# A new prologue for a one-core hybrid decoder layer: parameter loads on another queue, paired column tiles, 32-bit gate rows

## The chip, the cores and the metric

The kernel runs on 1 core of one Trainium2 chip. The metric is the device time of one execution in microseconds; 3 runs of the kernel before gave a median of 978.57 (978.53 to 978.91). Below, TensorE is the matmul engine (PE, its weight loads PEld), VectorE is DVE, ScalarE is ACT, GpSimd is POOL and SyncE is SP; SPq and ACTq are the DMA issues of those engines. PSUM has 8 banks of 512 columns in float32.

## The reference

One layer, with x of 1024 rows by 1024 columns:

```python
mod = jax.nn.silu(c) @ w_ada + b_ada
shift, scale, gate = jnp.split(mod, 3, axis=-1)
h = x * (1.0 + scale[:, None, :]) + shift[:, None, :]
proj = h @ w_in + b_in           # q,k,v,z | q,k,v,o,z | i,f | merge gates
# branch A: causal stick-breaking attention, 8 heads x 64, SiLU gate, projection
# branch B: conv on q,k, chunkwise mLSTM, 4 heads x 128, with i and log f per row
log_f = jax.nn.log_sigmoid(ml_f.astype(jnp.float32)).transpose(0, 2, 1)
y = (jax.nn.sigmoid(g_sb) * y_sb + jax.nn.sigmoid(g_ml) * y_ml) @ w_out
return layer_norm(DEEPNORM_ALPHA * x + (1.0 + gate[:, None, :]) * y, ln_g, ln_b)
```

What matters here is the start: the columns of mod (a product of a 1024 vector with 2048 columns of w_ada), h transposed (features on partitions), and the first products of h with w_in, among them 8 rows for the gates i and f of the four mLSTM heads.

## The kernel before

All large products are split into three: a number is kept as a high part (fp32r, 32 bits rounded by the copy) and a low part (the rest), and hH x wH, hL x wH and hH x wL are summed in a bank. The feature axis is cut into 8 tiles of 128 (KT), named d or k; the rows into two halves of 512. Every engine has its own program, written by hand, with semaphores between them. An engine works strictly in the order of its program.

The prologue, to about 70 us, does the following for each tile d:

- SP (lines 423 to 463) issues the load of x's 128 columns (x_rows), two loads of 128 columns of w_ada (a_raw, shift and scale; three slots, A_BUFS), and pieces of the first weights: load g (pro_load) is 4 of the 8 feature tiles of group g % 3; group 0 is the 8 gate columns, 1 and 2 are sb_q and sb_k. Load 3 and later wait until VectorE has made the low part of load g - 3. Ahead of all this stand seven small parameter loads (prm).
- VectorE (ada_rows, L1333 to L1339) sums silu(c)[k] times a_raw's row k over k, in two accumulators of 256 columns, and adds them.
- TensorE (ada_columns, L653) turns the sum over partitions into a column by a product with ones; VectorE (mod_columns, L1368 and L1369) adds the bias.
- TensorE (turn_x, L665) transposes x, 8 blocks into two banks; ScalarE (shifted, L941 and L945) applies scale and shift into h_raw (two buffers) and makes hH; VectorE (low_h, L1362) makes hL.
- TensorE (tile_of, L615 to L617) adds tile k's products into six banks: three groups, two halves, three products each. Group 0 has only 8 output rows (w_proH, w_proL with 8 columns).
- ScalarE and VectorE split each weight load into high part (L925) and low part (L1354), in pro_split(g).

TensorE's order is turn_x(d), tile_of(d - 1) of groups 0 and 1, ada_columns(d + 1), tile_of(d - 1) of group 2. After the last tile ScalarE moves the gate rows (r_if, L958), SP copies them to 4 partition groups with four loads of r_f and four of r_i (L467 and L469), and a chain of ScalarE and VectorE work on the rows begins. ScalarE then moves next_q and next_k out of the banks. The following products (project, L637) are jobs 3 and 4, then the loop over the four heads; job 3 writes the bank that next_q is read from.

## Time and profile before

| | |
|---|---|
| median of 3 runs | 978.57 us (978.53 to 978.91) |
| profiled execution | 978.23 us, of it the span 976.4 us |
| TensorE busy | 941.4 us (96%) |
| VectorE, ScalarE, GpSimd busy | 599.7 (61%), 454.3 (47%), 166.9 us (17%) |
| moved | 73.96 MB, mean 76 GB/s |
| chain that ended last | PE 83%, DVE 9%, the rest 2% or less each |

The page divides the span into 40 slices: TensorE is at 9 tenths in all but the first and the last, the DMA engines are at 9 in the first two only. In a timeline a row merges instructions of one kind that follow each other (x says how many): its two numbers are the start and the time from the first one's start to the last one's end. Matmuls are pipelined: one lasts some 0.4 us, but the next starts 0.23 us later, so starts are compared, not durations.

### The profile page before, as it was taken

The numbers are of one execution on the slowest core, as the hardware profiler recorded it, in microseconds if no ns is written. First come the engines' busy times: TensorE is split into PE (matmuls) and PEld (weight loads), VectorE is DVE, ScalarE is ACT, GpSimd is POOL, SyncE is SP. The second block draws the span as 40 slices with busy tenths as digits, with TensorE's granted clock in tenths as the row PEclk, the third lists the DMA queues.
The fourth block names the chain that finished last, engine by engine and source line by source line (L and its number), as shares of the span: only waits on it lengthen the run. The fifth ranks groups of instructions, "written<-read, shape, count | busy, mean of one in ns | idle before, by whom it ended". The sixth has DMA issues, their size and how long they took to land.

```text
span 976.4 us, 13097 instructions
## 1 busy us (share of the span) xinstructions
PE 941.4 (96%) x4965; PEld 757.3 (78%) x4965; DVE 599.7 (61%) x1144; ACT 454.3 (47%) x813; POOL 166.9 (17%) x138
## 2 busy tenths in 40 slices
PE   1999999999999999999999999999999999999996
PEld 1677878888778888778888778788888888878885
DVE  4857785666775757866657857543653333345996
ACT  2454575553665544665644756433843232242100
POOL 1010122240132430123220133311100000001200
PEclk9999999999999999999999999999999999999999
DMA  9932211102202012111113101115721221315232
GB/s 230 291 92 56 68 30 44 33 23 67 74 23 55 22 44 79 42 44 34 35 31 98 44 22 45 33 44 188 243 65 43 57 63 45 96 44 183 87 130 86
DMA packets 99561, 73.96 MB, mean 76 GB/s; under 512 B 4616, under 2 KB 90760, under 8 KB 99500
## 3 DMA queue, kind: packets, MB, share of 16 engines
q1 hardware_dynamic: 94828, 58.44, 22.2%
q0 software_dynamic: 2368, 8.41, 2.6%
q10 hardware_dynamic: 2304, 6.29, 1.7%
q8 instruction: 39, 0.64, 0.3%
q14 instruction: 22, 0.18, 0.1%
HBM read 64.59 MB, written 8.40 MB: 75 GB/s over the span
## 4 chain that ended last, share of the span: by engine, by line
PE 83%; DVE 9%; SPq 2%; ACT 2%; DMA 2%; issue 1%; DVEq 0%; ACTq 0%
PE bank L637 41%; PE bank L617 9%; PE bank L615 9%; PE bank L616 9%; PE bank L758 4%; PE bank L742 3%; DMA a_raw<-in_w_ada 2%; PE bank L731 2%; DVE m_q L1548 2%; DVE wL L1345 1%; PE bank L771 1%; SPq L454 1%; DVE m_q L1560 1%; PE bank L714 1%; PE bank L732 1%
## 5 line engine op out<-in xcount | busy, mean ns | idle before, releaser
L637 PE MATMUL bank<-hH,wH 128*128 128x512 f32 x688 | 274.8, 399 | 0.6 <-DVE wL L1345 0.6
L637 PE MATMUL bank<-hL,wH 128*128 128x512 f32 x688 | 272.9, 397 | 0.0
L637 PE MATMUL bank<-hH,wL 128*128 128x512 f32 x688 | 269.2, 391 | 0.0
L575 POOL TENSOR_TENSOR ez<-ez,rem 128x512 f32<-128x512 f32 (+3 forms) x96 | 136.0, 1436 | 411.2 <-DVE rem L1497 411.2
L637 PEld LDWEIGHTS bank<-hH,wH 128*128 128x128 f32 x688 | 129.1, 188 | 38.4 <-issue 10.7
L1345 DVE SCALAR_TENSOR_TENSOR wL<-w_raw,wH 128x512 fp32r<-128x512 f32 x116 | 87.6, 760 | 114.1 <-ACT wH L917 113.6
L637 PEld LDWEIGHTS bank<-hH,wL 128*128 128x128 f32 x688 | 129.4, 188 | 26.6
L637 PEld LDWEIGHTS bank<-hL,wH 128*128 128x128 f32 x688 | 129.4, 188 | 24.6 <-issue 1.0
L917 ACT ACTIVATE wH<-w_raw 128x512 fp32r<-128x512 f32 x116 | 72.5, 627 | 98.0 <-PE bank L617 71.1
L1497 DVE TENSOR_TENSOR_SCAN rem<-rem,ones 128x512 f32<-128x512 f32 (+3 forms) x96 | 88.6, 964 | 38.7 <-ACT rem L1019 38.7
L1006 ACT ACTIVATE ez<-bank 128x512 f32<-128x512 f32 (+3 forms) x96 | 41.8, 488 | 95.2 <-PE bank L733 95.2
L1481 DVE TENSOR_SCALAR ez<-ez 128x512 f32<-128x512 f32 (+3 forms) x80 | 27.5, 344 | 53.7 <-ACT ez L1006 52.7
L616 PE MATMUL bank<-hL,wH 128*128 128x512 f32 x144 | 56.2, 390 | 0.0
L615 PE MATMUL bank<-hH,wH 128*128 128x512 f32 x144 | 56.2, 390 | 0.0
L617 PE MATMUL bank<-hH,wL 128*128 128x512 f32 x144 | 56.0, 389 | 0.0
L1015 ACT ACTIVATE rem<-ez 128x512 f32<-128x512 f32 (+3 forms) x96 | 45.0, 517 | 7.2 <-DVE ez L1484 7.1
L604 POOL TENSOR_TENSOR yL<-yT,yH 128x1024 fp32r<-128x1024 f32 x4 | 9.6, 2396 | 207.5 <-ACT yH L1274 207.5
L1019 ACT ACTIVATE rem<-rem 128x512 f32<-128x512 f32 (+3 forms) x96 | 44.4, 510 | 0.0
L1027 ACT ACTIVATE at<-bank 128x512 f32<-128x512 f32 (+3 forms) x96 | 41.2, 482 | 5.6 <-PE bank L742 5.6
L758 PE MATMUL bank<-at,v_tok 128*64 128x128 f32 x576 | 42.0, 281 | 0.0
L742 PE MATMUL bank<-ident,ez 128*128 128x128 f32 x288 | 39.2, 272 | 0.0
L742 PEld LDWEIGHTS bank<-ident,ez 128*128 128x128 f32 x288 | 34.3, 140 | 6.1
(240 smaller groups left out, 1517.6 us busy)
## 6 DMA issues: line engine op xcount, KB each, us to landing
w_raw<-in_w_in SPq DMA_DIRECT2D x104, 256.0 KB, 2.9
a_raw<-in_w_ada SPq DMA_DIRECT2D x16, 512.0 KB, 7.3
x_rows<-in_x SPq DMA_DIRECT2D x8, 512.0 KB, 6.4
raw<-in_w_ada POOLq DMA_DIRECT2D x8, 512.0 KB, 4.7
x_in<-in_x SPq DMA_DIRECT2D x8, 512.0 KB, 4.2
out_y<-res SPq DMA_DIRECT2D x7, 512.0 KB, 2.9
raw<-in_w_out SPq DMA_DIRECT2D x10, 256.0 KB, 3.9
m_w<-bm_scratch ACTq DMA_DIRECT2D x4, 512.0 KB, 4.0
```

What stands on the lines that cost most here:

```text
L575: g.tensor_tensor(e, e, r, ALU.mult).then_inc(a_done[h], 1)
L615: t.matmul(ps, aH, bH, start=k == 0, stop=False)
L616: t.matmul(ps, aH, bL, start=False, stop=False)
L617: return t.matmul(ps, aL, bH, start=False, stop=k == kt - 1)
L637: ins = t.matmul(banks(number)[half][:], w, a, start=(r == 0), stop=(r == JOB_MM // 2 - 1))
L742: ins = t.transpose(z_ps[h][:, b * P:(b + 1) * P], ez[s % 2][h][:, b * P:(b + 1) * P], ident[:])
L758: ins = t.matmul(y_ps[64 * h:64 * h + 64, tt], v_tok[:, j, 64 * h:64 * h + 64], at_sb[h][:, b * P:(b + 1) * P], start=b == 0 and not conti ...
L917: a.activation(wH[:, slot, :, 0:width], w_raw[:, slot, :, 0:width], ACT.Copy, scale=scale)\
L1015: a.activation(rem[s % 2][h][:, 0:w], ez[s % 2][h][:, 0:w], ACT.Ln, bias=1.0).then_inc(ln_done[h], 1)
L1019: a.activation(r, r, ACT.Exp, scale=-1.0).then_inc(rem_done[h], 1)
L1345: v.scalar_tensor_tensor(out=wL[:, slot, :, 0:width], in0=w_raw[:, slot, :, 0:width], scalar=scale, in1=wH[:, slot, :, 0:width], op0=ALU.m ...
L1497: v.tensor_tensor_scan(back, back, ones[:, 0:1].to_broadcast((P, w)), first, ALU.mult, ALU.min)\
```

## The change

- The seven parameter loads are issued by ScalarE ahead of its table load, no longer by SP.
- The tiles form five blocks, [0], [1], [2, 3], [4, 5], [6, 7]. x and w_ada are loaded by block: 256 columns at a time for the pairs, w_ada in two pieces of four k each. ada_rows, ada_columns and mod_columns work by block, 512 wide for a pair.
- The gate rows (group 0) are no longer split products: w_if holds the 8 columns for all k, and gate_rows(d) multiplies them with h_raw in 32 bits, one product for each half; the halves' results stand in one bank, at partitions 0 to 7 and 32 to 39 (two column groups).
- low_h moves between the halves of a block's sums; the low parts of weight loads 3 to 5 are made behind mod_columns of block 2. TensorE's order is new.
- VectorE copies half 1 of the gate rows to partitions 0 to 7 before ScalarE adds the bias. The four r_i loads are issued by ScalarE, right behind r_if and ahead of next_q; the four r_f loads stay on SP.

The new `gate_rows`, the block loops and the orders, from the diff (`ada_pieces(b)` gives number, slot and k range of a block's pieces; `ada_freed(n)` is the count of sums that frees piece n's slot; `pro_slot(g)` only renumbers buffers):

```diff
 PRO_CHUNKS = 2 * PRO_K
+BLOCKS = [[0], [1], [2, 3], [4, 5], [6, 7]]
+BLOCK_OF = [b for b, tiles in enumerate(BLOCKS) for _ in tiles]
 A_BUFS = 3
...
-        pro_ps = [[y_ps[0:2 * NH, :], misc_ps[2][0:2 * NH, :]],
+        pro_ps = [[y_ps[32 * half:32 * half + 2 * NH, :] for half in range(2)],
                   [proj_ps[half][:] for half in range(2)], [z_ps[half][:] for half in range(2)]]
...
+            for b, tiles in enumerate(BLOCKS):
+                cols_b = slice(tiles[0] * P, (tiles[-1] + 1) * P)
+                sp.dma_start(x_rows[:, :, cols_b], x_v[:, :, cols_b]).then_inc(x_cols_in[b], 16)
+                for number, slot, lo, hi in ada_pieces(b):
+                    if number >= A_BUFS:
+                        sp.wait_ge(ada_used, ada_freed(number))
+                    piece = a_raw[:, slot].rearrange("p (k w c) -> p k w c", k=hi - lo, w=2)
+                    for what in range(2):
+                        sp.dma_start(piece[:, :, what], w_ada_w[:, lo:hi, what, cols_b]).then_inc(a_in[slot], 16)
+                for g in {0: range(3), 2: range(3, PRO_CHUNKS)}.get(b, ()):
+                    pro_load(g)
...
-                pe.wait_ge(x_cols_in[d], 16)
+                b = BLOCK_OF[d]
+                pe.wait_ge(x_cols_in[b], 16)
+                pe.wait_ge(mod_done, 2 * BLOCKS[b][-1] + 2)
...
+            def gate_rows(d):
+                for n in range(2):
+                    pe.wait_ge(m_drained[n], d + 2 - n)
+                if d % 4 == 0:
+                    pe.wait_ge(wL_done, PRO_K * (d // 4) + 1)
+                for half in range(2):
+                    ins = t.matmul(pro_ps[0][half], w_if[:, d], h_raw[:, d % 2, halves(half)], start=d == 0,
+                                   stop=d == KT - 1, skip_group_check=True)
+                    if d == KT - 1:
+                        ins.then_inc(filled[half], 1)
+                    elif half:
+                        ins.then_inc(if_used, 1)
...
             ada_columns(0)
-            for d in range(KT):
-                turn_x(d)
-                if d:
-                    tile_of(d - 1, 0, PRO_K - 1)
+            turn_x(0)
+            gate_rows(0)
+            for d in range(2):
+                tile_of(d, 1)
+                ada_columns(d + 1)
+                tile_of(d, 2)
+                turn_x(d + 1)
+                gate_rows(d + 1)
+            for d in range(2, KT):
                 if d + 1 < KT:
-                    ada_columns(d + 1)
-                if d:
-                    tile_of(d - 1, PRO_K - 1, PRO_K)
-            tile_of(KT - 1, 0, PRO_K)
+                    turn_x(d + 1)
+                tile_of(d, 1)
+                tile_of(d, 2)
+                if d % 2 == 0 and d + 2 < KT:
+                    ada_columns(d // 2 + 2)
+                if d + 1 < KT:
+                    gate_rows(d + 1)
...
                 if d > 1:
                     act.wait_ge(hL_done, d - 1)
+                    act.wait_ge(if_used, d - 1)
...
-                        bias_copy(r_if[0:2 * NH, halves(half)], half, n,
-                                  r_bias[0:2 * NH, :], pro_ps[0][half])
+                        else:
+                            act.wait_ge(if_moved, 1)
+                        rows = r_if[0:2 * NH, halves(half)]
+                        bias_copy(rows, half, n, r_bias[0:2 * NH, :], rows if half else pro_ps[0][half])
...
                         pro_split(g)
+                if n == 0:
+                    for half in range(2):
+                        act.wait_ge(drained[half], 1)
+                    for q in range(4):
+                        act.dma_start(r_i[32 * q:32 * q + NH, :], r_if[0:NH, :]).then_inc(rows_in, 16)
...
+            ada_rows(0, 0, KT)
+            mod_columns(0)
+            for g in range(3):
+                pro_split(g)
+            for b in range(1, len(BLOCKS)):
+                ada_rows(b, 0, KT // 2)
+                low_h(b - 1 if b < 3 else 2 * b - 4)
+                ada_rows(b, KT // 2, KT)
+                if b > 2:
+                    low_h(2 * b - 3)
+                mod_columns(b)
+                if b == 2:
+                    for g in range(3, PRO_CHUNKS):
                         pro_split(g)
-                elif d < 4:
-                    pro_split(d + 2)
-            low_h(KT - 1)
+            for d in range(KT - 2, KT):
+                low_h(d)
+            dve.wait_ge(filled[1], 1)
+            dve.wait_ge(rows_zero, 5)
+            v.tensor_copy(r_if[0:2 * NH, halves(1)], pro_ps[0][1]).then_inc(if_moved, 1)
```

How the instructions stand, at three places. First VectorE, from the low part of tile 1 to that of tile 2. The kernel before (a_raw the columns of w_ada, a_acc their sums, ada_in the slots' loads):

```order
L1362 TENSOR_TENSOR hL<-h_raw,hH 128x1024 [waits hH_done]
L1368 TENSOR_TENSOR mod<-bank,cols 128x1 [waits ada_done]
L1369 SCALAR_TENSOR_TENSOR mod<-bank,cols 128x1
L1354 SCALAR_TENSOR_TENSOR w_proL<-w_raw,w_proH 128x512 [waits wH_done]
L1333 TENSOR_SCALAR a_acc<-a_raw,silu_c 128x256 [waits ada_done,ada_in0]
L1333 TENSOR_SCALAR a_acc<-a_raw,silu_c 128x256
L1336 SCALAR_TENSOR_TENSOR a_acc<-a_raw,silu_c,a_acc 128x256 [waits ada_used] x6
L1339 TENSOR_TENSOR a_acc<-a_acc 128x256 [waits ada_used]
L1362 TENSOR_TENSOR hL<-h_raw,hH 128x1024 [waits hH_done]
```

The change, from the fifth of the eight wide sums (tiles 2 and 3):

```order
L1395 SCALAR_TENSOR_TENSOR a_acc<-a_raw,silu_c,a_acc 128x512 [waits ada_used,ada_in0]
L1395 SCALAR_TENSOR_TENSOR a_acc<-a_raw,silu_c,a_acc 128x512 [waits ada_used] x3
L1400 TENSOR_TENSOR a_acc<-a_acc 128x512 [waits ada_used]
L1430 TENSOR_TENSOR mod<-bank,cols 128x1 [waits ada_done]
L1432 SCALAR_TENSOR_TENSOR mod<-bank,cols 128x1
L1430 TENSOR_TENSOR mod<-bank,cols 128x1
L1432 SCALAR_TENSOR_TENSOR mod<-bank,cols 128x1
L1414 SCALAR_TENSOR_TENSOR w_proL<-w_raw,w_proH 128x512 [waits wH_done] x2
L1392 TENSOR_SCALAR a_acc<-a_raw,silu_c 128x512 [waits ada_in1,ada_done]
L1392 TENSOR_SCALAR a_acc<-a_raw,silu_c 128x512
L1395 SCALAR_TENSOR_TENSOR a_acc<-a_raw,silu_c,a_acc 128x512 [waits ada_used] x2
L1424 TENSOR_TENSOR hL<-h_raw,hH 128x1024 [waits hH_done]
```

hL of tile 2 (the last row of both) stood behind the sums of tile 3 alone; it now stands behind the low parts of loads 4 and 5 (the row x2) and half of the sums of tiles 4 and 5. The low part of load 5 waits for wH_done, which ScalarE gives. hL of tile 1 now stands ahead of these rows, behind the fourth wide sum.

Second ScalarE, in the change alone, from tile 0's hH to tile 3's h_raw:

```order
L994 ACTIVATE hH<-h_raw 128x1024 [waits misc_drained1,misc_drained0]
L974 ACTIVATE w_if<-w_raw 128x32 [waits weights_in0]
L990 ACTIVATE h_raw<-bank,mod 128x512 [waits misc_filled0,mod_done]
L990 ACTIVATE h_raw<-bank,mod 128x512 [waits misc_filled1]
L994 ACTIVATE hH<-h_raw 128x1024 [waits misc_drained1,misc_drained0]
L974 ACTIVATE w_proH<-w_raw 128x512 [waits weights_in1]
L990 ACTIVATE h_raw<-bank,mod 128x512 [waits if_used,misc_filled0,hL_done,mod_done]
L990 ACTIVATE h_raw<-bank,mod 128x512 [waits misc_filled1]
L994 ACTIVATE hH<-h_raw 128x1024 [waits misc_drained1,misc_drained0]
L974 ACTIVATE w_proH<-w_raw 128x512 [waits weights_in2]
L990 ACTIVATE h_raw<-bank,mod 128x512 [waits if_used,misc_filled0,hL_done,mod_done]
```

At the end of the prologue, in the change:

```order
L1007 ACTIVATE r_if<-bank,r_bias 8x512 [waits proj_filled0,rows_zero,bias_in]
L1007 ACTIVATE r_if<-r_if,r_bias 8x512 [waits proj_filled1,if_moved]
L1043 DMA r_i<-r_if 4x1024 [waits proj_drained1,proj_drained0]
L1043 DMA r_i<-r_if 4x1024 x3
L1007 ACTIVATE next_q<-bank,cols 128x512 [waits proj_filled0]
L1007 ACTIVATE next_q<-bank,cols 128x512 [waits proj_filled1]
L1007 ACTIVATE next_k<-bank,cols 128x512 [waits proj_filled0]
```

The kernel before has the same rows up to h_raw of tile 3. There load 3 (w_if here, w_proH there) was issued right behind the columns of tile 1; it now stands behind the loads of the whole pair. At the end, these stood behind each other before:

```order
L958 ACTIVATE r_if<-bank,r_bias 8x512 [waits proj_filled0,rows_zero,bias_in]
L958 ACTIVATE r_if<-bank,r_bias 8x512 [waits proj_filled1]
L958 ACTIVATE next_q<-bank,cols 128x512 [waits proj_filled0]
L958 ACTIVATE next_q<-bank,cols 128x512 [waits proj_filled1]
L958 ACTIVATE next_k<-bank,cols 128x512 [waits proj_filled0]
L958 ACTIVATE next_k<-bank,cols 128x512 [waits proj_filled1]
```

Four DMA issues came in between r_if and next_q.

Third TensorE. The kernel before, the end of tile 1 to the start of tile 2:

```order
L616 MATMUL bank<-hL,w_proH 128x512
L617 MATMUL bank<-hH,w_proL 128x512
L665 MATMUL bank<-ident,x_rows 128x128 [waits mod_done,x_cols_in2]
L665 MATMUL bank<-ident,x_rows 128x128 x3
L665 MATMUL bank<-ident,x_rows 128x128 [waits misc_drained1]
L665 MATMUL bank<-ident,x_rows 128x128 x3
L615 MATMUL bank<-hH,w_proH 8x512 [waits hL_done]
L616 MATMUL bank<-hL,w_proH 8x512
L617 MATMUL bank<-hH,w_proL 8x512
```

The change, the same stretch (L678 transposes, L689 gate rows, L627 to L629 split products, L666 column sums):

```order
L629 MATMUL bank<-hH,w_proL 128x512
L678 MATMUL bank<-ident,x_rows 128x128 [waits misc_drained0,mod_done,x_cols_in2]
L678 MATMUL bank<-ident,x_rows 128x128 x3
L678 MATMUL bank<-ident,x_rows 128x128 [waits misc_drained1]
L678 MATMUL bank<-ident,x_rows 128x128 x3
L689 MATMUL bank<-h_raw,w_if 8x512 [waits misc_drained1,misc_drained0]
L689 MATMUL bank<-h_raw,w_if 8x512
L678 MATMUL bank<-ident,x_rows 128x128 [waits misc_drained0,mod_done,x_cols_in2]
L678 MATMUL bank<-ident,x_rows 128x128 x3
L678 MATMUL bank<-ident,x_rows 128x128 [waits misc_drained1]
L678 MATMUL bank<-ident,x_rows 128x128 x3
L627 MATMUL bank<-hH,w_proH 128x512 [waits hL_done]
L628 MATMUL bank<-hL,w_proH 128x512
```

Transposes and gate rows of tile 2 and transposes of tile 3 now come before the first split product of tile 2.

## Rows read from the trace of the kernel before

**Rows 1.** The page, busy us, share of the span, instructions.
```profile
PE 941.4 (96%) x4965; PEld 757.3 (78%) x4965; DVE 599.7 (61%) x1144; ACT 454.3 (47%) x813; POOL 166.9 (17%) x138
```

**Rows 2.** Waits, TensorE, 66 to 240 us: total us, times, longest.
```profile
PE bank L637 <- DVE wL L1345: 0.6, 1, 0.6
```

**Rows 3.** DMA view, 0 to 100 us: busy tenths in 40 slices of 2.5.
```profile
DMA  0199999999999999999999100041153000302240
```

**Rows 4.** Windows: length, busy us of each engine, clock, DMA share, GB/s.
```profile
45.00:50.00 5.00, 5.00 (x30) 3.86 (x28) 4.26 (x13) 1.99 (x4) 0.00 (x0) 1.00 1.17 291
...
944.00:948.00 4.00, 4.00 (x19) 3.21 (x18) 2.59 (x4) 0.00 (x0) 0.00 (x0) 1.00 0.77 260
```

**Rows 5.** Timeline, SP's DMA issues: start us, us, what.
```profile
0.81 0.41 SPq L431 DMA_DIRECT2D prm<-in_c  x1
...
3.48 0.43 SPq L450 DMA_DIRECT2D x_rows<-in_x  x1
```

**Rows 6.** Timeline, VectorE at the start; in brackets idle time and what ended it.
```profile
7.00 0.17 DVE L1321 TENSOR_TENSOR silu_c<-cols,small 128x8 f32<-128x8 f32 x1
...
11.39 0.61 DVE L1333 TENSOR_SCALAR a_acc<-a_raw,silu_c 128x256 f32<-128x256 f32 x2 [4.22 <-DMA a_raw<-in_w_ada]
...
19.02 0.62 DVE L1333 TENSOR_SCALAR a_acc<-a_raw,silu_c 128x256 f32<-128x256 f32 x2 [1.55 <-DMA a_raw<-in_w_ada]
```

**Rows 7.** Timeline, TensorE: tile 0, tile 2, the one wait, job 3.
```profile
26.11 0.63 PE L616 MATMUL bank<-hL,w_proH 128*8 128x512 f32 x1
...
26.54 0.63 PE L617 MATMUL bank<-hH,w_proL 128*8 128x512 f32 x1
...
37.48 0.48 PE L615 MATMUL bank<-hH,w_proH 128*8 128x512 f32 x1
...
41.60 0.61 PE L653 MATMUL bank<-ones,a_acc 128*128 128x1 f32 x4 [1.08 <-DVE a_acc L1339]
...
69.30 0.39 PE L637 MATMUL bank<-hH,wH 128*128 128x512 f32 x1
```

**Rows 8.** Timeline, TensorE, tile 4: transposes, gate products, first 128-wide.
```profile
49.06 1.04 PE L665 MATMUL bank<-ident,x_rows 128*128 128x128 f32 x8
49.85 0.48 PE L615 MATMUL bank<-hH,w_proH 128*8 128x512 f32 x1
...
51.31 0.40 PE L615 MATMUL bank<-hH,w_proH 128*128 128x512 f32 x1
```

**Rows 9.** DMA issues, 0 to 100 us: count, KB each, median us to landing.
```profile
r_bias<-in_b_in POOLq DMA_DIRECT2D x1, 0.0 KB, 4.6
```

**Rows 10.** Timeline, VectorE's and ScalarE's steps for a tile and a load.
```profile
27.76 0.62 ACT L925 ACTIVATE w_proH<-w_raw 128x512 fp32r<-128x512 f32 x1
...
49.56 2.46 DVE L1336 SCALAR_TENSOR_TENSOR a_acc<-a_raw,silu_c,a_acc 128x256 f32<-128x256 f32 x6
...
49.78 1.45 ACT L941 ACTIVATE h_raw<-bank,mod 128x512 f32<-128x512 f32 x2 [2.92 <-PE bank L665]
51.32 1.06 ACT L945 ACTIVATE hH<-h_raw 128x1024 fp32r<-128x1024 f32 x1
...
52.41 1.23 DVE L1362 TENSOR_TENSOR hL<-h_raw,hH 128x1024 fp32r<-128x1024 f32 x1
...
64.55 1.89 DVE L1345 SCALAR_TENSOR_TENSOR wL<-w_raw,wH 128x512 fp32r<-128x512 f32 x3
```

**Rows 11.** Timeline, TensorE: 32-bit products in two column groups, and the next.
```profile
403.28 0.44 PE L758 MATMUL bank<-at,v_tok 128*64 128x128 f32 x4
403.65 0.45 PE L731 MATMUL bank<-kH,qH 64*128 64x384 f32 x2
```

**Rows 12.** Timeline, the gate rows' copies and issues; ScalarE's own DMA issue.
```profile
66.09 1.29 ACT L958 ACTIVATE r_if<-bank,r_bias 8x512 f32<-8x512 f32 x2 [1.15 <-PE bank L617]
...
70.08 2.44 SPq L469 DMA_DIRECT2D r_i<-r_if  x4
...
107.93 0.34 ACTq L1139 DMA_DIRECT2D m_w<-bm_scratch  x1
```

More of the change, by code:

```diff
@@ L127, with pro_slot, ada_pieces, ada_freed @@
 PRO_CHUNKS = 2 * PRO_K
+BLOCKS = [[0], [1], [2, 3], [4, 5], [6, 7]]
+BLOCK_OF = [b for b, tiles in enumerate(BLOCKS) for _ in tiles]
 A_BUFS = 3
 Y_BUFS = 4
+def pro_slot(g):
+    return (g // PRO_K) * (PRO_K - 1) + g % PRO_K - 1
+def ada_pieces(b):
+    if b < 2:
+        return [(b, b, 0, KT)]
+    return [(2 * b - 2 + part, (2 * b - 2 + part) % A_BUFS, part * KT // 2, (part + 1) * KT // 2) for part in range(2)]
+def ada_freed(number):
+    before = number - A_BUFS
+    return 8 * (before + 1) if before < 2 else 16 + 4 * (before - 1)
 def segments():
@@ L467, in _ @@
                 sp.dma_start(r_f[32 * q:32 * q + NH, :], r_if[NH:2 * NH, :]).then_inc(rows_in, 16)
-            for q in range(4):
-                sp.dma_start(r_i[32 * q:32 * q + NH, :], r_if[0:NH, :]).then_inc(rows_in, 16)
             off = dict(zip(("mlq", "mlk", "mlv", "mlo", "mlz"), OFF_ML)) |\
@@ L905, in _ @@
             a = nc.scalar
+            bi = b_in[0]
+            rows = [
+                (ROW_C, c[0]), (ROW_ADA, b_ada[0]), (ROW_B, bi[0:OFF_IF]),
+                (ROW_GSB, bi[OFF_GSB:OFF_GSB + 2 * D]), (ROW_CB, conv_b[0]), (ROW_NG, ml_norm_g[0]),
+            ]
+            for row, src in rows:
+                src = src.rearrange("(t p) -> t p", p=P)
+                act.dma_start(prm[row:row + src.shape[0], :], src).then_inc(params_in, 16)
+            act.dma_start(prm[ROW_CW:ROW_CW + 4 * KT, :], conv_w[0].rearrange("j (t p) -> (j t) p", p=P))\
+                .then_inc(params_in, 16)
             a.preload_act_table_set("natural_log_exp_and_others")
@@ L987, in _ @@
                         pro_split(g)
+                if n == 0:
+                    for half in range(2):
+                        act.wait_ge(drained[half], 1)
+                    for q in range(4):
+                        act.dma_start(r_i[32 * q:32 * q + NH, :], r_if[0:NH, :]).then_inc(rows_in, 16)
                 if n == 2:
@@ L1323, in _, with ada_rows @@
             dve.wait_ge(silu_done, 1)
-            def ada_rows(d):
-                dve.wait_ge(a_in[d % A_BUFS], 32 * (d // A_BUFS + 1))
-                if d > 1:
-                    dve.wait_ge(ada_done, d - 1)
-                for k in range(KT):
-                    acc, row = a_acc[:, d % 2, k % 2], a_raw[:, d % A_BUFS, k]
+            def ada_rows(b, lo, hi):
+                if lo == 0 and b > 1:
+                    dve.wait_ge(ada_done, b - 1)
+                width = len(BLOCKS[b]) * P
+                for k in range(lo, hi):
+                    for number, slot, first, _ in ada_pieces(b):
+                        if k == first:
+                            dve.wait_ge(a_in[slot], 32 * (number // A_BUFS + 1))
+                    acc, row = a_acc[:, b % 2, k % 2, :, 0:width], ada_rows_of(b, k)
                     if k < 2:
```

125 lines of the change are left out of this document (52 added, 73 removed).

## Prediction

> **What bounds the kernel now.** I read the page first: TensorE is busy nearly all of the span of 976.4 us, so a change of its prologue counts by how much later or earlier TensorE starts its steady work [rows 1]. I take "job 3" (the first product of L637, at 69.30) as the end of the prologue and ask when it starts in the changed kernel. From the waits of TensorE behind it comes one more term, 0.6 us for VectorE's wL (L1345) [rows 2].
>
> Next the DMA digits and the windows: from 5 to about 54 us the DMA engines are saturated [rows 3], at 290 GB/s with rows of 512 bytes [rows 4]. SP issues the seven parameter loads first; x starts at 3.48 instead of 0.81 [rows 5]. The first two column tiles of w_ada are in at 11.39 and 19.02; silu(c) had been ready since 7.2 [rows 6]. Then TensorE: its products begin at 25.5, at first 0.43 us apart where later ones are 0.233 apart, as the lower of its two clock levels, 1.2 GHz, would give; tile 2 begins at 37.48, and between there and 69.30 it waits only once, for 1.1 us at 41.6 (the load of tile 4) [rows 7]. So from tile 2 on the prologue is 31.8 us of almost solid TensorE work. One tile of it: transposes 0.79, six 8-wide gate products 1.46 (0.233 each, and 0.06 that the first waits behind the transposes), twelve 128-wide ones 2.8, column sums about 0.5 [rows 7, 8].
>
> **The change, part by part.**
>
> *Parameters on ScalarE.* The big loads start 2.67 us earlier (0.81 for 3.48) [rows 5]. The parameters now travel beside them. Lower end: they are in as before. Upper end: r_bias, which did travel beside them, took 4.6 us to land [rows 9]; issued until 3.4, they are in at 8.0, silu(c) at 10.2, 1.5 us after tile 0's columns (11.39 - 2.67 = 8.7). The chain below has 1 to 2 us of slack there (ScalarE waits for a load until 26.2), so I price it at 0, at most 1.
>
> *Pairs.* Tiles 2 and 3 become one block. Tile 1's columns are in at 19.02 - 2.67 = 16.3. Behind them come x of two tiles and two pieces of w_ada, 3 x 1.05 MB. At 290 GB/s this takes 10.9 us. Rows of 1024 bytes may go faster: at 4 KB rows the engines moved 260 GB/s at a share of 0.77, 338 per unit of share, against 290/1.17 = 248 [rows 4]. I take 340 GB/s, between 290 and 395 (338 x 1.17), nearer to 512 bytes: 9.3 us, second piece in at 25.6; ends 24.3 and 27.2. The row shows that longer rows are cheaper. The Trainium skill ("DMA: Bandwidth & Descriptors", Specifications) asks for 512 B or more for line rate; by that rule the pairs would gain nothing and my sum would be 1.6 us higher. The trace disagrees in part: 512-byte rows stay at 290.
>
> *The chain to tile 2's products.* The third gate load (16 KB) is queued behind both pieces, and ScalarE's w_if copy of it stands in front of tile 1's h_raw: about 26.2. Then ScalarE: copy 0.3, h_raw 1.55, hH 1.15 (with gaps) -> 29.2 [rows 10]. VectorE has low_h(1) ahead of the second half of the block's sums: 1.14; four wide steps. A 256-wide step is 0.41, a 512-wide operation of the same kind 0.63 [rows 10]; at 0.66 four are 2.6; the wide final sum 0.7 (low_h, 1024 wide, takes 1.22) -> 33.6. TensorE's columns and the four mod operations 1.2 -> 34.9, while TensorE does tile 1's second product (1.4) -> transposes of tile 2 at 35.9. Then 0.7, h_raw 1.55, hH 1.15 -> 39.3, and now the order of the change matters: VectorE has mod, then the low part of weight load 5, then the first half of the next block, and only then low_h(2). Load 5's high part stands on ScalarE behind hH(2): 0.62 -> 39.95; VectorE 0.7, two wide TENSOR_SCALARs 0.42 and two steps 0.66 (2.2), low_h(2) 1.3 -> **44.1**. Before, tile 2 began at 37.5: 6.6 us later. Both waits can be read in the order of the instructions, they are no estimate; TensorE idles some 3.5 us here.
>
> *TensorE from tile 2 to job 3.* Six tiles x 12 x 0.233 = 16.8; four sets of transposes 3.5; two sets of eight column sums 1.2; one wait for VectorE's sums 0.6; five gate rows. A gate row is two 32-bit products, 512 wide, in two column groups. The nearest row is L758: two such products, 128 wide, are followed by the next work after 0.37 us [rows 11]; a 128-wide 32-bit transpose takes 0.79/8 = 0.10 [rows 8], and each of the two rounds is 384 columns longer (0.32): 1.0, with the change of mode 1.1. Lower end 0.95 (no such loss), upper end no overlap at all, 1.95. The row shows two groups starting together. The Trainium skill ("TensorEngine Tiling (Array Packing)", Key Properties) says that a change of tiling mode drains the engine; without any drain the sum would be 0.1 us less a row. Five rows: 5.5. Together 27.6 against 31.8: **-4.2**.
>
> *Copy of the rows, r_i on ScalarE's queue.* Gate row 7 now ends 2.8 us before job 3 could start (call that J), the rows' chain moves up. But ScalarE has, in this order: three weight copies until J - 2.35, r_if half 0 and half 1 (0.65 each) until J - 1.0, four r_i issues, and only then next_q, whose bank job 3 writes. An issue of r_i takes 0.58 + 0.04 on SP, 2.44 for four; ScalarE's own issue of m_w took 0.34 [rows 12]. With 0.61: J + 1.5, next_q's first half 0.7 (and 0.1) -> J + 2.3. TensorE waits **+2.3**; with 0.34 each, +1.2.
>
> *Behind it.* The rows' chain reaches VectorE relatively 3 us earlier, so the wait of 0.6 for wL goes [rows 2]: **-0.6**. The two others of 0.6 and 0.7 in the first iteration are VectorE's conv work, which follows TensorE: 0.
>
> **Sum:** 6.6 - 4.2 + 2.3 - 0.6 = +4.1 us. Against the profiled execution's 978.23 it is 982.3; the median of the runs is 0.34 above that, so 982.7.
>
> **Rivals.**
> 1. *The pairs cost by number, not by size* (the other side). Where a wide VectorE operation costs what a narrow one does, the four steps, the sum and the next block's half take 1.75 us less, and with loads at 395 GB/s another 1.3: tile 2 at 41.0, sum +1.0, 979.6. This mechanism makes the kernel faster where tile 2 starts before 40.0 (37.5 + 4.2 - 2.3 + 0.6); with tile 2 at 38.0, hardly later than before, the sum is 0.5 - 4.2 + 2.3 - 0.6 = -2.0, 976.6. For it: a narrow operation has a fixed share in its 0.41. Against it: the 1024-wide one takes 1.22, and the two waits that the order fixes are left. 8 in 100 for all of it.
> 2. *No wait at job 3*: ScalarE's issues are cheap or next_q is early: 1.2 to 2.3 less, 980.4 to 981.6. For it the row of 0.34, against it that r_i's shape cost 0.58. 15 in 100.
> 3. *The column groups do not overlap*, 1.95 instead of 1.1 a gate row, five times: +4.2, 986.9. Against it: L758's pairs. 8 in 100.
> 4. *Loads gain nothing from longer rows* (the rule above, here as a mechanism): second piece and third gate load 1.6 us later, 984.3. 15 in 100.
> 5. *TensorE falls to the slower clock* in its idle stretches before 44: each product then costs 0.2 more for a few us: +1 to +2, 984.2. For it: tile 0's products 0.43 apart after an idle stretch. 10 in 100.
> The forecast itself: 44 in 100.
>
> **How the numbers follow.** The likeliest time is 982.7. A measurement of this kernel tells about 0.2% from no change, 976.6 to 980.5. Faster: the far end of rival 1, 0.06. Within: the rest of 1, the low part of 2, and errors of the chain of over 2 us, 0.15. Slower 0.79. The range of 979.0 to 987.0 takes in rivals 2 to 5 and leaves out most of rival 1 and combinations of 3 with 4 or 5.
>
> **What would show it.** The third gate load's copy on ScalarE near 26; VectorE waiting some 4 us for wH of load 5, until about 40; tile 2's first product (L627) near 44; gate rows of 1.1 us (start to next start); four r_i issues on ScalarE ahead of next_q, and L649's first product 2 us after L629's last; behind it no wait for wL. The forecast is wrong if tile 2 starts before 41, or if the gate rows cost below 0.8 us.

## The result, and the profile after

| | before | changed |
|---|---|---|
| median of the runs | 978.55 us (978.26 to 978.91) | 986.31 us (984.98 to 987.99) |
| single runs, granted clock | all within 0.7 us | 985.02 (0.993), 984.98 (0.993), 987.60 (0.990), 987.99 (0.986) |
| profiled execution, its span | 978.23, 976.4 us | 985.02, 983.3 us |
| job 3 starts | 69.30 | 77.02 |

The change makes the kernel slower: the ratio of the times is 1.0082, 95% interval 1.0069 to 1.0094. The runs of the kernel before agree to 0.07%; those of the changed kernel are 3 us apart, the slower ones with the lower mean clock of TensorE. The profiled execution, on which the readings below rest, is one of the two faster runs.

The page of the changed kernel, busy us, share of the span, instructions; this answers to [rows 1]:

```profile
PE 942.7 (96%) x4949; PEld 755.7 (77%) x4949; DVE 596.4 (61%) x1116; ACT 454.1 (46%) x813; POOL 167.0 (17%) x138
```

TensorE is busy 1.3 us longer, though it has fewer instructions; the rest of the 6.9 us by which the span grew is idle time. Job 3 comes 7.7 us later, so all of the loss lies in the prologue, and 0.8 us came back behind it. The windows of the prologue (us, busy us of PE, PEld, DVE, ACT, POOL, granted clock, DMA share, GB/s), against 290 GB/s in [rows 4]:

```profile
20.00:30.00 10.00, 7.45 (x30) 5.16 (x28) 5.82 (x13) 3.25 (x5) 0.00 (x0) 1.00 1.13 329
30.00:40.00 10.00, 6.68 (x28) 5.14 (x28) 4.71 (x11) 1.45 (x2) 0.00 (x0) 0.83 1.10 348
40.00:50.00 10.00, 6.40 (x27) 4.49 (x27) 8.30 (x12) 4.08 (x5) 0.00 (x0) 0.83 0.61 190
50.00:60.00 10.00, 10.00 (x57) 6.96 (x56) 7.27 (x16) 5.02 (x6) 0.00 (x0) 1.00 0.17 51
```

While they run the loads are faster. They stand still from 42 to 45 us (0 GB/s in windows of 1 us), where SP waits for a slot of a_raw, and end near 52, where those of [rows 3] went on to 55. TensorE is idle for a third of the time from 30 to 50, and its clock is 0.83 there. One caution on the clock column: up to about 24 us it reads 1.00 although tile 0's products are 0.43 us apart (20.71 to 23.44), and it does so in the kernel before too; in that stretch the spacing tells the level and the column does not. TensorE's rows of that stretch (start, us, what, in brackets the idle time before it and what ended it), for [rows 7]:

```profile
33.84 1.05 PE L666 MATMUL bank<-ones,a_acc 128*128 128x1 f32 x8 [1.71 <-DVE a_acc L1400]
34.76 0.65 PE L627 MATMUL bank<-hH,w_proH 128*128 128x512 f32 x1
...
37.34 1.51 PE L678 MATMUL bank<-ident,x_rows 128*128 128x128 f32 x8
40.11 1.03 PE L689 MATMUL bank<-h_raw,w_if 128*8 128x512 f32 x4 [1.25 <-ACT h_raw L990]
...
45.66 0.79 PE L627 MATMUL bank<-hH,w_proH 128*128 128x512 f32 x1 [3.50 <-DVE hL L1424]
...
48.39 0.47 PE L627 MATMUL bank<-hH,w_proH 128*128 128x512 f32 x1
...
50.73 1.03 PE L689 MATMUL bank<-h_raw,w_if 128*8 128x512 f32 x4
51.70 1.09 PE L678 MATMUL bank<-ident,x_rows 128*128 128x128 f32 x8
...
77.02 0.47 PE L649 MATMUL bank<-hH,wH 128*128 128x512 f32 x1 [2.36 <-ACT next_q L1007]
```

Tile 2 starts at 45.66 (37.48 before), behind 3.50 us of waiting for hL; the six products from 34.76 (to 37.34) and the first six of tile 2 (to 48.39) are 0.43 us apart, the spacing of the lower clock; a gate row takes 0.97 us (50.73 to 51.70); job 3 waits 2.36 us for next_q. VectorE and ScalarE say why hL of tile 2 is late:

```profile
35.20 0.68 DVE L1414 SCALAR_TENSOR_TENSOR w_proL<-w_raw,w_proH 128x512 fp32r<-128x512 f32 x1
41.66 0.69 DVE L1414 SCALAR_TENSOR_TENSOR w_proL<-w_raw,w_proH 128x512 fp32r<-128x512 f32 x1 [5.78 <-ACT w_proH L974]
42.27 0.87 DVE L1392 TENSOR_SCALAR a_acc<-a_raw,silu_c 128x512 f32<-128x512 f32 x2
43.07 1.40 DVE L1395 SCALAR_TENSOR_TENSOR a_acc<-a_raw,silu_c,a_acc 128x512 f32<-128x512 f32 x2
44.39 1.22 DVE L1424 TENSOR_TENSOR hL<-h_raw,hH 128x1024 fp32r<-128x1024 f32 x1
...
40.05 1.06 ACT L994 ACTIVATE hH<-h_raw 128x1024 fp32r<-128x1024 f32 x1
41.02 0.61 ACT L974 ACTIVATE w_proH<-w_raw 128x512 fp32r<-128x512 f32 x1
```

VectorE stands 5.78 us at the low part of load 5, whose high part ScalarE makes only behind hH of tile 2, then works on the next block, and only then makes the hL that TensorE waits for. At the other end of the prologue:

```profile
72.66 0.73 ACT L1007 ACTIVATE r_if<-r_if,r_bias 8x512 f32<-8x512 f32 x1
73.47 2.68 ACTq L1043 DMA_DIRECT2D r_i<-r_if  x4
73.74 2.76 SPq L481 DMA_DIRECT2D r_f<-r_if  x4
76.19 1.27 ACT L1007 ACTIVATE next_q<-bank,cols 128x512 f32<-128x512 f32 x2 [2.81 <-issue]
80.68 1.06 ACT L1046 ACTIVATE r_e<-r_f 128x1024 f32<-128x1024 f32 x1 [2.06 <-DMA r_f<-r_if]
```

The four r_i issues keep ScalarE for 2.7 us, 0.67 each (0.61 on SP in [rows 12]). The rows are in 7.3 us after r_if ends at 73.39; before it was 6.9 us (67.38 to 74.25). Two queues brought nothing here; why the second queue did not help is not shown.

### The profile page after: what moved, and what is told of

It reads as the page before. It is cut to its first block, busy times and chain, and to the rows that moved or that the text cites. A ratio compares the mean times of both kernels' runs of the same rounds, so it can differ in the third digit from the quotient of the medians.

```text
span 983.3 us, 13050 instructions
## 1 busy us (share of the span) xinstructions
PE 942.7 (96%) x4949; PEld 755.7 (77%) x4949; DVE 596.4 (61%) x1116; ACT 454.1 (46%) x813; POOL 167.0 (17%) x138
## 4 chain that ended last, share of the span: by engine, by line
PE 85%; DVE 10%; ACT 3%; issue 1%; ACTq 1%; DMA 1%; POOL 0%; DVEq 0%; POOLq 0%
PE bank L649 42%; PE bank L627 9%; PE bank L629 9%; PE bank L628 9%; PE bank L792 4%; PE bank L776 3%; PE bank L765 2%; DVE m_q L1619 1%; PE bank L805 1%; DVE m_q L1631 1%; DVE wL L1405 1%; PE bank L748 1%; PE bank L766 1%; PE bank L767 1%; PE bank L810 1%
## 5 line engine op out<-in xcount | busy, mean ns | idle before, releaser
L649 PEld LDWEIGHTS bank<-hH,wH 128*128 128x128 f32 x688 | 129.1, 188 | 40.2 <-issue 13.5
L627 PE MATMUL bank<-hH,wH 128*128 128x512 f32 x144 | 56.2, 390 | 0.0
L629 PE MATMUL bank<-hH,wL 128*128 128x512 f32 x144 | 56.0, 389 | 0.0
```

What stands on the lines that cost most here:

```text
L627: t.matmul(ps, aH, bH, start=k == 0, stop=False)
L629: return t.matmul(ps, aL, bH, start=False, stop=k == kt - 1)
L649: ins = t.matmul(banks(number)[half][:], w, a, start=(r == 0), stop=(r == JOB_MM // 2 - 1))
```

## The experiments

All times are medians. The experiments ran on four chips; the kernel before, run beside each of them, had 978.15 to 978.40 us, so medians from different chips can be compared to some 0.4 us. An interval is given where the comparison is with the kernel before.

### The changed kernel, one cause at a time

**r_i back on SP.**

```diff
+            for q in range(4):
+                sp.dma_start(r_i[32 * q:32 * q + NH, :], r_if[0:NH, :]).then_inc(rows_in, 16)
...
-                    for q in range(4):
-                        act.dma_start(r_i[32 * q:32 * q + NH, :], r_if[0:NH, :]).then_inc(rows_in, 16)
```

> The changed kernel, with the four r_i issues back on SP behind the four of r_f. Theory (the issues stand ahead of next_q and cost TensorE its 2.36 us wait at job 3; the rows arrive no later, since 6.9 us passed between r_if and the rows before and 7.3 us now): the wait for next_q at L649 falls below 0.3 us, the rows are in at most 0.5 us later, a wait for wL of up to 0.7 us may come back; 1.5 to 2.4 us faster than the changed kernel, some 984.2 us. Rival (TensorE has a second reason to wait there, or the rows' chain becomes late): the wait moves to another line and less than 1 us is gained.

Measured: 982.87 us (982.43 to 988.47), ratio to before 1.0059 [1.0038, 1.0081]; the median is 3.4 us below the changed kernel's, more than expected. Four runs have a clock of 0.994 (982.4 to 985.0); the profiled one, 988.47, has 0.990. The wait for next_q is gone. In its place, the timeline of ScalarE and TensorE some 15 us later, and the window behind it:

```profile
82.91 1.06 ACT L1043 ACTIVATE r_e<-r_f 128x1024 f32<-128x1024 f32 x1 [5.07 <-DMA r_i<-r_if]
...
92.34 0.50 PE L651 MATMUL bank<-hH,wH 128*128 128x512 f32 x1 [1.86 <-DVE wL L1402]
```

```profile
92.00:96.00 4.00, 3.66 (x11) 2.93 (x12) 3.93 (x6) 0.00 (x0) 0.00 (x0) 0.67 0.25 66
```

The rows arrive as late as with two queues, 7.3 us after r_if (75.57 to 82.91). But the wait for wL is 1.86 us, where at most 0.7 was expected, and the clock behind it is 0.67. So by the waits of this one profile the issues cost TensorE 2.36 us and hid 1.86, and undoing them alone is worth 0.5 us. The runs show more: three of them lie at 982.4 to 982.9 where the changed kernel's two best have 985.0, at nearly the same mean clock. This isn't settled, since mean clocks do not say where the slow stretches lay.

**Low parts of loads 3 to 5 behind block 3.**

```diff
-                if b == 2:
+                if b == 3:
                     for g in range(3, PRO_CHUNKS):
                         pro_split(g)
```

> The changed kernel, with the low parts of weight loads 3 to 5 made behind mod_columns of block 3 instead of block 2, so that hL of tile 2 no longer stands behind the wait for load 5's high part. Theory (this order fixes tile 2's start at 45.66): tile 2 starts at 42 to 42.8, some 3 us earlier, and the kernel gains 2.7 to 3.4 us, up to 4.5 if TensorE then stays at the higher clock; about 983 us. Rival (tile 2 waits for the loads, the sums or h in any case): tile 2 starts later than 44.5 and less than 1.2 us is gained. Second rival (the low parts of loads 3 to 5 then come too late for tile 4's products): a wait at tile 4's first product takes back over 1 us.

Measured: 984.07 us (980.47 to 984.38), 2.2 us faster than the changed kernel where 2.7 to 3.4 were expected. The profiled run, 980.47 at a clock of 0.995, is 4.5 us faster than the changed kernel's profiled one; the other three have 0.988 and 984.0 to 984.4. TensorE's timeline:

```profile
29.77 0.72 PE L627 MATMUL bank<-hH,w_proH 128*128 128x512 f32 x1 [1.28 <-DVE hL L1424]
30.30 0.63 PE L628 MATMUL bank<-hL,w_proH 128*128 128x512 f32 x1
30.72 0.63 PE L629 MATMUL bank<-hH,w_proL 128*128 128x512 f32 x1
...
40.23 0.50 PE L627 MATMUL bank<-hH,w_proH 128*128 128x512 f32 x1 [0.26 <-DVE hL L1424]
```

Tile 2 starts at 40.23, 5.4 us earlier, with 0.26 us of waiting for 3.50; the rival (it waits in any case) falls, and no wait at tile 4 takes its place. The shorter wait alone makes 3.2 us. The rest is the clock: tile 1's second products and the transposes behind them were at the higher level here (1.6 us), and the clock had risen earlier in tile 0, so that tile 1's h_raw starts 0.7 us earlier. Tile 1's first products, on the other hand, were at the lower level (30.30 to 30.72), behind the same 1.28 us wait behind which the changed kernel kept the higher one (at 30.46).

**Fillers against the clock.**

```diff
+            def fill(n):
+                for _ in range(n):
+                    t.matmul(misc_ps[2][:], w_proH[:, 0, 0], hH[:, 0, halves(0)], start=True, stop=True,
+                             skip_group_check=True)
```

> The changed kernel, with 31 more 512-wide products (8 rows of nothing that is read: they go into a bank that no one reads then) in TensorE's idle stretches of the prologue: 6 before the column sums of tiles 2 and 3, 4 before each of two pairs of gate rows and 4 behind one, 13 before the first product of tile 2. Nothing else moves. Theory (part of the prologue's time is the lower clock that TensorE is granted behind its idle stretches, 0.43 us a product instead of 0.233): the products of tile 1 and of tile 2 run 0.23 apart, the kernel gains 1.5 to 2.9 us although it does more, and its runs lie closer together than the 3 us of the changed kernel's; about 984 us. Rival (the lower clock only fills time in which TensorE would wait for VectorE anyway, and the fillers stand in the way): no change or up to 2 us slower.

The fillers are full 128-row products. Measured: 984.05 us, four runs from 983.79 to 984.28, clock 0.995 in each. It does 31 products more and is 2.3 us faster at the median; the spread of 3 us is gone. Profile against profile it is only 0.7 us faster (984.28 against 985.02). Windows, and then TensorE's timeline at the two starts:

```profile
30.00:40.00 10.00, 9.20 (x50) 6.56 (x50) 4.61 (x12) 3.02 (x4) 0.00 (x0) 1.00 1.10 349
40.00:50.00 10.00, 9.22 (x48) 6.52 (x47) 9.96 (x19) 2.54 (x4) 0.00 (x0) 1.00 0.79 242
...
70.00:80.00 10.00, 7.64 (x27) 5.80 (x26) 1.92 (x4) 5.24 (x8) 0.00 (x0) 0.83 0.41 92
```

```profile
43.87 0.50 PE L627 MATMUL bank<-hH,w_proH 128*128 128x512 f32 x1 [0.48 <-DVE hL L1433]
...
74.52 0.47 PE L649 MATMUL bank<-hH,wH 128*128 128x512 f32 x1 [2.36 <-ACT next_q L1016]
```

At the higher clock tile 2 starts at 43.87 and job 3 at 74.52, within 0.5 us of what the prediction's chain gives (44.1 and 74.0). Behind the 2.36 us wait at job 3, which had no filler, the clock now fell (0.83), which it did not in the changed kernel's profile. From job 3 to the end of the span it is 907.9 us here and 906.3 there: 1.6 of the 2.5 us that job 3 gained are lost again. The changed kernel's profile is the exception: in all four other profiles with that wait (low parts behind block 3, fillers, one column group, parameters on SP) job 3's first products are 0.43 us apart, and it is 907.8 to 907.9 us from there to the end.

**Both halves of a gate row in one column group.**

```diff
-        pro_ps = [[y_ps[32 * half:32 * half + 2 * NH, :] for half in range(2)],
+        pro_ps = [[y_ps[0:2 * NH, :], misc_ps[2][0:2 * NH, :]],
```

> The changed kernel, with the two halves of the gate rows in two banks, both at partitions 0 to 7, so that the two products of a gate row are in the same column group. Theory (two column groups run side by side, 0.96 us for two products at the higher clock): now 1.75 to 1.95 us a gate row, six of the eight of them on TensorE's critical path: 4 to 6 us slower than the changed kernel, some 991 us. Rival (the groups do not overlap, a 32-bit product of 8 rows takes 0.48 us by itself): no change.

Measured: 989.46 us (987.65 to 990.77), 3.2 us slower than the changed kernel. TensorE's start of tile 2, then a gate row and what follows it:

```profile
44.20 0.79 PE L627 MATMUL bank<-hH,w_proH 128*128 128x512 f32 x1 [2.65 <-DVE hL L1424]
...
56.39 1.88 PE L689 MATMUL bank<-h_raw,w_if 128*8 128x512 f32 x4
58.21 1.09 PE L678 MATMUL bank<-ident,x_rows 128*128 128x128 f32 x8
```

1.82 us for 0.96: the two column groups do run side by side. Five rows behind tile 2's start make 4.3; from there to the end of the prologue it is 34.8 us instead of 29.0, of which another 1.2 is six more products at the lower clock. The median grew by less than the 4 to 6 expected; the clocks of the two sets of runs differ.

This profile also tells the clock from the fillers. It has no fillers, and tile 1's h_raw starts when it does in the changed kernel (26.65 for 26.56), but its clock is 1.00 from 30 to 40 us where the changed kernel's is 0.83. Tile 2 then starts at 44.20, 1.46 us earlier and within 0.1 us of the prediction's 44.1.

**Parameter loads back on SP.**

```diff
+                sp.dma_start(prm[row:row + src.shape[0], :], src).then_inc(params_in, 16)
...
-                act.dma_start(prm[row:row + src.shape[0], :], src).then_inc(params_in, 16)
```

> The changed kernel, with the seven parameter loads back on SP, ahead of x. Theory (in the changed kernel the DMA queue never runs dry, so the big loads' 2.67 us count in full up to tile 2): x goes out at 3.48, tile 2 starts 2 to 2.7 us later (near 48), the kernel is 2 to 2.7 us slower than the changed one, 987 to 990. Rival (as from the kernel before, where the same move brought 0.4 us): no difference.

Measured: 989.46 us (988.16 to 991.67, clocks 0.986 to 0.991), 3.2 us slower than the changed kernel. x goes out at 3.46, tile 2 starts at 48.29 instead of 45.66, 2.63 us later. The number is the expected one, but not all of it comes from the loads. First the changed kernel's rows (TensorE turning the parameters into columns, then ScalarE's h_raw of tile 1), then this kernel's h_raw of tile 1, TensorE's column sums and transposes of tile 2, and its first product:

```profile
8.39 0.45 PE L658 MATMUL bank<-ident,prm 128*128 128x128 f32 x1 [8.39 <-DMA prm<-in_conv_w]
...
26.56 1.45 ACT L990 ACTIVATE h_raw<-bank,mod 128x512 f32<-128x512 f32 x2 [0.71 <-PE bank L678]
```

```profile
28.17 1.43 ACT L990 ACTIVATE h_raw<-bank,mod 128x512 f32<-128x512 f32 x2
...
35.44 1.86 PE L678 MATMUL bank<-ones,a_acc 128*128 128x1 f32 x8 [0.45 <-DVE a_acc L1400]
37.16 0.77 PE L639 MATMUL bank<-hH,w_proH 128*128 128x512 f32 x1
...
39.87 1.91 PE L690 MATMUL bank<-ident,x_rows 128*128 128x128 f32 x8
...
48.29 0.50 PE L639 MATMUL bank<-hH,w_proH 128*128 128x512 f32 x1 [1.77 <-DVE hL L1424]
```

The copy of load 3, the load that ScalarE needs ahead of that h_raw, comes 2.4 us later (28.03 for 25.62). But h_raw starts only 1.6 us later, because in the changed kernel it did not wait for the load: ScalarE stood 0.71 us for TensorE's transposes of tile 1. The column sums then start 1.6 us later too (35.44 for 33.84) and take 1.72 us for 0.92: the clock is 0.50 from 30 to 40 us here. So of the 2.63 us some 1.6 are the loads and 1.0 is the clock, and in the changed kernel the 2.67 us do not count in full.

### The kernel before, one part of the change at a time

**Parameters on ScalarE alone.** (The diff is the reverse of the last.)

> The kernel before, with only the seven parameter loads moved from SP to ScalarE, ahead of its table load. Theory (the tile loads set tile 2's start, and they go out 2.67 us earlier, while silu(c) gets later only up to 10.4 us, as it did in the changed kernel): tile 2 starts near 34.8, job 3 near 66.6 instead of 69.3; 2.2 to 2.7 us faster than before, about 976. Rival (tile 0's sums start only 0.8 us earlier, and the chain of tile 0 sets the rest): 0 to 1 us faster.

Measured: 977.85 us (977.38 to 978.53), ratio 0.9996 [0.9986, 1.0005]: nothing clear of the noise, and the theory was wrong. SP's issues in the timeline, and the window from 10 to 20:

```profile
7.67 2.81 SPq L442 DMA_DIRECT2D a_raw<-in_w_ada  x2
15.78 0.37 SPq L428 DMA_DIRECT2D w_raw<-in_w_in  x1
16.19 0.51 SPq L438 DMA_DIRECT2D x_rows<-in_x  x1
```

```profile
10.00:20.00 10.00, 2.95 (x12) 2.50 (x12) 8.49 (x26) 4.16 (x8) 0.00 (x0) 1.00 0.86 217
```

SP stands from 10.5 to 15.8 at load 3, which waits for VectorE's low part of load 0; that is made behind tile 0's columns (15.56), and these come no earlier than silu(c) lets them. The DMA engines run dry (75 and 4 GB/s from 15 to 16 and from 16 to 17), tile 2's x goes out at 16.19 (16.71 before), and tile 2 starts 0.5 us earlier. The kernel before has the same stop at load 3, but a shorter one, from 13.5 to 16.3.

**The same, with loads 3 to 5 one tile later**, so that SP isn't stopped.

```diff
-                elif d < 4:
-                    pro_load(d + 2)
+                elif 1 < d < 5:
+                    pro_load(d + 1)
...
```

> The kernel before with the parameter loads on ScalarE, and loads 3 to 5 of the weights issued one tile later (their copies and low parts as well). Theory (with the parameters moved alone, SP stood at load 3 until 15.8 us, waiting for VectorE's low part of load 0 behind tile 0's columns, and the DMA engines ran dry; that took back all but 0.5 of the 2.67 us): SP issues tile 2's x by 11, 200 to 220 GB/s between 10 and 20 us become over 260, tile 2 starts 1.5 to 2.5 us earlier than before's 37.48, job 3 near 67, 1.5 to 2.5 us faster than before, about 976.3. Rival (the sums of tile 0 cannot start before 10.9 since the parameters are in late, and that is what sets it): within 0.7 us of before.

Measured: 975.79 us (975.57 to 976.42), ratio 0.9975 [0.9966, 0.9985], faster than before. The queue stays full, in the timeline and in the window:

```profile
10.41 2.01 SPq L438 DMA_DIRECT2D x_rows<-in_x  x1
...
66.67 0.39 PE L625 MATMUL bank<-hH,wH 128*128 128x512 f32 x1
```

```profile
10.00:20.00 10.00, 2.95 (x12) 2.49 (x12) 8.43 (x26) 3.98 (x7) 0.00 (x0) 1.00 1.17 290
```

Tile 2 starts at 35.99, job 3 at 66.67, 2.63 us earlier. Of the 2.4 us, the parameters' move alone gives 0.4, within the noise; the other 2.0 come with the later loads 3 to 5. What these would bring with the parameters left on SP was not run.

**32-bit gate rows alone**, with gate_rows(d) behind tile d - 1's last group:

```diff
-                    tile_of(d - 1, 0, PRO_K - 1)
+                    tile_of(d - 1, 1, PRO_K - 1)
...
+                gate_rows(d)
```

> The kernel before, with only the gate rows as 32-bit products in two column groups (with VectorE's copy of half 1; single tiles, parameters and r_i on SP as before; gate_rows(d) stands behind the last group of tile d - 1). Theory (a gate row is 0.96 us for 1.46, which counts only where TensorE and not the load is the bound, tiles 4 to 7, and the rows' chain starts 2.8 us earlier, so the 0.6 us wait for wL goes): 1.5 to 3.5 us faster than before, about 976. Rival (the loads, one tile in 5.4 us, take TensorE's place as the bound at once): at most 1 us faster.

Measured: 978.60 us (978.32 to 980.08), ratio 1.0008 [0.9998, 1.0017]: no gain. The wait for wL is 1.64 us instead of 0.60. **With the parameters on ScalarE as well:**

> The kernel before with both: parameters on ScalarE and the 32-bit gate rows, but single tiles and r_i on SP. Theory (these two are the parts of the change that help, and the pairs with their order and the r_i issues are what costs): 4 to 6 us faster than before, about 973.5. Rival (the gain is lost to a wait at the end of the prologue or to the lower clock of TensorE): under 2 us.

Measured: 978.57 us (977.65 to 979.91), ratio 1.0004 [0.9995, 1.0014]. TensorE now waits for VectorE's sums at tile after tile, and again for wL:

```profile
26.66 0.61 PE L643 MATMUL bank<-ones,a_acc 128*128 128x1 f32 x4 [1.10 <-DVE a_acc L1362]
...
83.19 0.50 PE L627 MATMUL bank<-hH,wH 128*128 128x512 f32 x1 [1.88 <-DVE wL L1368]
```

Both rivals hold: the loads take TensorE's place as the bound (VectorE's sums in turn wait 0.3 to 2.2 us for a_raw at tiles 2 to 6), and what job 3 gains (67.55 for 68.54 with the parameters alone) the wait for wL takes back (1.88 for 0.65).

### Repairs

**The changed kernel with three repairs:** r_i on SP, low parts behind block 3, 18 fillers ahead of tile 2 (the edits shown above).

> The changed kernel with all three repairs: r_i issues back on SP, low parts of loads 3 to 5 behind block 3's columns, and 18 products that no one reads in TensorE's idle stretches ahead of tile 2. Theory (the three losses add up: 2.4 us at job 3, some 3.3 at tile 2, the lower clock 1.5 to 3): tile 2 near 40.5, job 3 near 68.5, no stretch at the lower clock behind 30, a wait for wL of 1 to 1.9 us at the fourth job, since the rows now arrive relatively late; 6 to 7.5 us faster than the changed kernel's median, 978.5 to 980, and its runs within 0.5 us of each other. Rival (the losses overlap, one repair makes the next wait longer): above 981.

Measured: 979.21 us (978.39 to 981.74), ratio 1.0011 [1.0001, 1.0020], 7.1 us faster than the changed kernel. The profiled run has tile 2 at 41.41, job 3 at 69.55, a clock of 1.00 from 20 to 80, and the expected wait for wL, 1.80 us. The three gains, 3.4, 2.2 and 2.3 us by the medians, nearly add up. Tile 2 and job 3 are 0.9 and 1.05 us later than expected; the last parameter load landed at 9.86 in this profile and at 8.71 in the next version's, which has tile 2 at 40.16 and job 3 at 68.28. Eight of ten runs lie within 1.4 us (0.5 was expected), two (981.3, 981.7, the latter the profiled one) have a lower clock.

**And the low part of load 9 ahead of the scans:**

```diff
                 link(v.tensor_tensor(r_f[:], r_f[:], r_e[:], ALU.min))
+                pro_split(PRO_CHUNKS + 3)
...
             row_logs()
-            pro_split(PRO_CHUNKS + 3)
```

> The changed kernel with the three repairs, and in addition the low part of weight load 9 made ahead of VectorE's two scans of the rows instead of behind them. Theory (the remaining wait of 1.8 us at the fourth job is VectorE's order, and the lower clock behind it follows from that idle stretch): no wait for wL, granted clock 1.00 between 80 and 100 us, 1.8 to 3 us faster than without it, 976.5 to 977.5, 1 to 2 us faster than the kernel before. Rival (the rows' chain, 0.7 us later, makes TensorE wait further on): under 1 us.

Measured: 978.14 us (977.38 to 978.63), 1.1 us faster, as fast as the kernel before (1.0001 [0.9991, 1.0010]). The wait for wL is gone, and TensorE waits further on for the rows themselves:

```profile
91.22 1.09 PE L717 MATMUL bank<-ident,r_q 128*128 128x128 f32 x8 [0.99 <-ACT r_q L1058]
```

The gain is less than the 1.8 to 3 expected, and the rival has half of it: behind job 3 the chain of the rows is a floor of its own.

**The best of the single-tile versions:** parameters on ScalarE, loads 3 to 5 later, 32-bit gate rows, early low part of load 9.

> The kernel before with the parameter loads on ScalarE, loads 3 to 5 one tile later, the 32-bit gate rows in two column groups, and the low part of load 9 ahead of the row scans (r_i on SP, single tiles). Theory (TensorE saves 0.5 us a tile, but a tile's loads take 5.4 us and its own work then 5.0, so TensorE waits for the sums of each tile; behind job 3 the chain of the rows is the floor, which these edits hardly move): 0 to 1.2 us faster than with the first two edits alone, 974.6 to 975.8. Rival (the gate rows pay in full once the queue does not run dry): 2 us or more faster, under 973.8. Second rival (TensorE, now waiting at each tile, falls to its lower clock in some runs): 976 or more in those.

Measured: 975.82 us (975.29 to 977.36), ratio 0.9974 [0.9965, 0.9984]; the version without the last two edits had 975.79. Job 3 starts at 66.12, 0.55 earlier, and TensorE then waits 1.0 us for r_q, the clock being 0.91 from 80 to 100. The gate rows bring nothing here either; four runs above 976.8 have clocks of 0.995 to 0.997, the other six 0.997 to 0.998, which leans to the second rival without showing it. Both beat the kernel before and the changed one.

## Why the prediction was right in sign and short in size

The forecast of 982.7 had the sign and the mechanism; the median is 986.31, near the upper end of the range. Its sum was made against the profiled execution: +4.1 us, measured +6.8 (978.23 to 985.02), and the other runs lie higher still.

- **Parameters at 0, big loads 2.67 us earlier: the sum came out, the path did not.** x goes out at 0.81, silu(c) is ready at 10.6 (10.2 was worked out). The price of 0 rested on slack: ScalarE would wait for a load until 26.2 and start tile 1's h_raw at 26.5. The load's copy was over at 25.85, and h_raw started at 26.56, behind TensorE's transposes, which follow from silu(c) through tile 0. So there was no slack; the late parameters cost 0.7 us here, and loads 0.6 us faster than worked out covered it. That h_raw started on time is luck. With the last parameter in at 9.32 instead of 8.39 (the profile with r_i back on SP) h_raw and tile 2 both start 0.7 us later. And of the 2.67 us about 1.6 reach tile 2, by the run with the loads back on SP; the same move in the kernel before brought 0.5. The likely reason for the difference is load 3, which the change also takes out of SP's way, between tiles 1 and 2; no run put it back in the changed kernel. The prediction saw load 3 only as something that ScalarE gets later.
- **Pairs at 340 GB/s: right.** 329 and 348 were measured, the gate load's copy started at 25.6 (26.2). Rival 4 falls, and with it the rule of the Trainium skill beside it ("DMA: Bandwidth & Descriptors", Specifications: 512 B or more for line rate): rows of 512 bytes gave 290 GB/s, rows of 1024 bytes 348.
- **The chain to tile 2: the two waits were right, the clock in it was not.** The wide steps came near the 0.66 counted (2.73 us for four), VectorE's sum was done at 33.8 (33.6), mod at 35.2 (34.9), VectorE stopped at load 5, and TensorE was idle for 3.50 us (3.5): each in its place. The step that failed is "TensorE does tile 1's second product (1.4) -> transposes of tile 2 at 35.9". The six products of that "second product" took 2.6 us, and the transposes came at 37.3 and were slow themselves: tile 2 at 45.66 for 44.1.
- **Tile 2 to job 3: 29.0 us for 27.6.** The first six products of tile 2 took 2.73 us for 1.40. The rest nearly cancels: gate rows were cheaper (0.96 for 1.1, 0.7 in all) and the wait of 0.6 for VectorE's sums did not come, but the two sets of column sums took 0.9 for 0.6, and the products, at 0.233 each but more where they follow or precede another kind, took 0.9 more in all. Rival 3 (no overlap) falls: one group for both halves makes it 1.82.
- **The four issues: right, +2.36 for +2.3.** Rival 2 falls. 0.67 us each is r_i's own price, the cheap issue of m_w (0.34) was the wrong neighbour.
- **-0.6 behind it: the number was right in this profile, the reason half.** 0.8 us came back. It was put down to rows that reach VectorE earlier. They do so only because TensorE waits 2.36 us: r_if ends 1.3 us before job 3 could have started (1.9 in the kernel before). With r_i back on SP the wait for wL is 1.86 us, so by the profiles +2.3 and -0.6 were one term, which could not be undone apart; the runs of that version gained more than this allows. And in the four other profiles with the wait at job 3 nothing came back, since the clock was low behind it.
- **Rival 5 was not a rival but came on top.** The lower clock cost 1.2 + 0.4 ahead of tile 2 and 1.3 behind its start, 2.9 us in the profiled run, and by their mean clocks more in the runs at 0.990 and 0.986. It was given 10 in 100 as a case of its own, though the chain it sits beside has TensorE idle 1.7, 1.25 and 3.5 us in any case. With the fillers the chain's times are met to 0.5 us, and without them, where the clock happened to stay up (one column group), tile 2 is met to 0.1. In the profiled run that is the whole miss of 2.7 us: the mis-sized term is the speed of TensorE's products in the stretch in which the prediction itself had it wait.

What stays open: the size of the gain of r_i on SP (0.5 us by the waits of one profile, 3.4 by the medians), and why the changed kernel's other two runs are 2.6 to 3.0 us above the profiled one. A lower clock behind job 3 (1.5 us) and later parameters are both seen in other profiles, but no profile shows these runs.

## What to carry to other kernels

Where a change makes a nearly always busy TensorE wait, price the products behind each wait at the lower clock as part of the forecast, and expect runs to differ; do not keep it as a separate case. Before an earlier transfer is counted, read what its queue stops at next: issuing the loads 2.67 us earlier brought 0.4 us, and 2.4 once loads 3 to 5, which wait for a buffer, were issued later. Where a term is priced at 0 because of slack, follow every path that ends at that point and not only the one expected to be last. And when an issue is put on a compute engine's queue, everything behind it waits: what then comes back from another wait may be the same time counted once more.
